# Attention output and its gate kept feature-major through to the output projection

## What is computed

```
h = rmsnorm(x, norm_w) * (1 + scale) + shift;   z = h @ w_in
q_lat, ckv, kr, g_att, u, g_pool = split(z)              # g_att is 512 wide
o[q, head, :] = softmax(q . k, causal) @ v               # 8 heads of 64 values
att = o reshaped to (2048, 512)
mixed = concat(att * silu(g_att), pool(u) * silu(g_pool))   # 1024 wide
y_prompt = rmsnorm(x + gate * (mixed @ w_out), final_norm_w)
```

## Time and profile before

| | us |
|---|---|
| runs (3) | 1607.35, 1608.68, 1615.50 |
| median | 1608.68 |
| span of the profiled execution | 1616.8 |
| PE matmul busy | 1483.7 (92%) |
| DVE, ACT, POOL busy | 780.6, 651.9, 493.5 |

### The profile page before, as it was taken

One profiled execution on the slowest core, in us unless ns is written; L12 is line 12 of the kernel. 1 busy time (PEld: TensorE's weight loads), 2 busy tenths in 40 slices (PEclk: granted clock), 3 DMA queues, 4 the chain that ended last, 5 costly groups with the idle time before them and its releaser, 6 DMA issues. The chain is left out here.

```text
span 1616.8 us, 24423 instructions
## 1 busy us (share of the span) xinstructions
PE 1483.7 (92%) x8584; PEld 1236.4 (76%) x8584; DVE 780.6 (48%) x1594; ACT 651.9 (40%) x1296; POOL 493.5 (31%) x423
## 2 busy tenths in 40 slices
PE   7787799999999589999999999999848999999997
PEld 1487689999998467777777787877627888888886
DVE  0587532223321677766676767664252333333333
ACT  0255322222110556565666666666631222222221
POOL 0355523232221524343443434343331111111100
PEclk9899899999999799999999999999957999999999
DMA  9243221111101200000000000000065144434310
GB/s 367 94 126 110 84 87 53 53 53 52 58 27 47 52 1 11 11 8 12 8 12 8 14 4 14 7 7 11 15 244 181 60 157 156 155 122 146 124 60 28
DMA packets 71502, 114.70 MB, mean 71 GB/s; under 512 B 33236, under 2 KB 50548, under 8 KB 69205
## 3 DMA queue, kind: packets, MB, share of 16 engines
q1 hardware_dynamic: 58782, 70.73, 13.8%
q0 software_dynamic: 3456, 27.26, 4.6%
q10 hardware_dynamic: 9168, 15.50, 2.7%
HBM read 90.95 MB, written 22.77 MB: 70 GB/s over the span
## 5 line engine op out<-in xcount | busy, mean ns | idle before, releaser
L1177 POOL TENSOR_TENSOR pt_lo<-pt,pt_hi 128x512 fp32r<-128x512 f32 (+2 forms) x160 | 171.1, 1069 | 262.3 <-ACT pt_hi L1082 261.9
L1081 ACT ACTIVATE pt<-att_ps_s 128x512 f32<-128x512 f32 (+1 forms) x320 | 170.2, 532 | 150.9 <-PE att_ps_s L1351 85.3
L1237 DVE TENSOR_REDUCE mx<-att_ps_p 128x1 f32<-128x512 f32 (+2 forms) x300 | 177.2, 606 | 91.7 <-PE att_ps_p L1321 71.4
L1082 ACT ACTIVATE pt_hi<-att_ps_s 128x512 fp32r<-128x512 f32 (+1 forms) x320 | 169.2, 529 | 0.0
L1248 DVE TENSOR_TENSOR pt_lo<-pt,pt_hi 128x512 fp32r<-128x512 f32 (+1 forms) x160 | 120.2, 751 | 93.0 <-ACT pt_hi L1082 91.2
L107 PE MATMUL mix_ps_u<-mix_h_hi,wb_hi 128*128 128x256 f32 x512 | 146.2, 285 | 0.0
L109 PE MATMUL mix_ps_u<-mix_h_hi,wb_lo 128*128 128x256 f32 x512 | 144.9, 283 | 0.0
L108 PE MATMUL mix_ps_u<-mix_h_lo,wb_hi 128*128 128x256 f32 x512 | 144.9, 283 | 0.0
L107 PE MATMUL att_ps_o<-pt_hi,v_hi 128*128 128x512 f32 (+1 forms) x320 | 126.9, 397 | 9.3 <-DVE pt_lo L1248 8.5
L107 PE MATMUL out_ps_y<-wo_hi,mixed_hi 128*128 128x512 f32 x256 | 119.4, 466 | 2.6 <-POOL mixed_lo L1938 2.6
L1349 PE MATMUL att_ps_s<-q_hi,k_hi 97*128 97x512 f32 (+1 forms) x320 | 120.3, 376 | 1.6 <-issue 1.6
(11 more groups left out here) (348 smaller groups left out, 3316.2 us busy)
## 6 DMA issues: line engine op xcount, KB each, us to landing
ada<-in_ada_w_dram SPq DMA_DIRECT2D x8, 1536.0 KB, 15.1
lat_x<-in_x_prompt_dram SPq DMA_DIRECT2D x16, 512.0 KB, 4.3
mix_x<-in_x_prompt_dram SPq DMA_DIRECT2D x16, 512.0 KB, 3.7
x_rows<-in_x_prompt_dram SPq DMA_DIRECT2D x16, 512.0 KB
out_dram<-y ACTq DMA_DIRECT2D x16, 512.0 KB, 2.7
lat_wraw<-in_w_in_dram POOLq DMA_DIRECT2D x8, 768.0 KB
gate_att_scratch<-gate_a SPq DMA_DIRECT2D x16, 256.0 KB, 2.0
pool_scratch<-mixed SPq DMA_DIRECT2D x32, 128.0 KB, 2.0
```

The costliest lines, as they stand in the source:

```text
L1081: act.activation(pt[:, k % 2, 0:n], ps_s[:, k % 2, 0:n], ACT.Exp, scale=SCALE)
L1082: act.activation(ph[0][:, k % 4, 0:n], ps_s[:, k % 2, 0:n], ACT.Exp, scale=SCALE).then_inc(exp_done, 1)
L1177: pool.tensor_tensor(ph[1][:, k % 4, 0:n], pt[:, k % 2, 0:n], ph[0][:, k % 4, 0:n].bitcast(F32), ALU.subtract).then_inc(p_lo_ready[1], 1)
L1237: dve.tensor_reduce(mx[:, I % 2, r, c:c + 1], chunk_bank(g, n)[:, 0:width], AX.X, ALU.max).then_inc(chunk_read, 1)
```

## The change

Nothing is transposed back to token-major any more.

- **mix**: `ps_a` becomes feature-major like `ps_u`. The two (token block) groups of 8 x 3 matmuls with 512 moving columns become, per step, 4 groups of 8 x 3 with 256 moving columns. The gate scratch is (4, 128, 2048) and SP writes it in rows of 1 KB.
- **attention**: `turn_out` and `finish` are gone, with their semaphores. `o_cols` has two buffers; ACT copies, after a wait for the store of two groups before, and SP stores 64 rows of values (unnormalised) and the one row of sums, two DMAs, into `att_scratch` (4, 128, 2048) and `den_scratch` (8, 2048). The reuse of the `ps_o` bank waits for ACT's copy.
- **setup**: SP first loads all sums as 128x128 (`s_den`), DVE takes one reciprocal of them, SP writes them back (`rden_scratch`) ahead of its other stores, for which it waits on DVE. The loads of the first block come after that; POOL does two multiplications.
- **output**: per block five DMAs instead of three, all in rows of 512 bytes (attention and pool columns into one tile `raw_cols`, gate columns, and the reciprocals spread over 64 partitions twice). POOL multiplies gate by reciprocal, then attention by that, and makes the whole low part (128x1024); ACT makes the whole high part in one instruction. PE's `turn` and DVE's `low` are gone.

The core of the diff:

```diff
-                    for c in range(KC):
-                        cols = slice(b * P, (b + 1) * P)
-                        last = mm3(pe, ps_a[:, b, :], [hb[0][:, e, c, cols], hb[1][:, e, c, cols]],
-                                   [wb[0][:, c, 0:DATT], wb[1][:, c, 0:DATT]], c == 0, c == KC - 1)
+                    for k in range(2):
+                        cols = slice((2 * b + k) * P, (2 * b + k + 1) * P)
+                        for c in range(KC):
+                            last = mm3(pe, ps_a[:, b, k * T:(k + 1) * T], [wb[0][:, c, cols], wb[1][:, c, cols]],
+                                       [hb[0][:, e, c, :], hb[1][:, e, c, :]], c == 0, c == KC - 1)
...
             def store(h, I):
-                sp.wait_ge(att_ready, NGRP * h + I + 1)
-                sp.dma_start(att_groups[:, I, :, ds(h, 1), :].squeeze(2), att[:, I % 2]).then_inc(att_out[I % 2], 16)
+                sp.wait_ge(ot_ready, NGRP * h + I + 1)
+                cols = slice(I * 512, (I + 1) * 512)
+                sp.dma_start(att_heads[:, ds(h, 1), cols], ot[0:VD, I % 2, :].unsqueeze(1)).then_inc(att_out[I % 2], 16)
+                sp.dma_start(den_heads[:, ds(h, 1), cols], ot[VD:VW, I % 2, :].unsqueeze(1)).then_inc(att_out[I % 2], 16)
...
-                if exists(NGRP * h + I - 1, NGRP * H):
-                    act.wait_ge(ot_turned, NGRP * h + I)
-                act.activation(ot[0:VW, :], ps_o[0:VW, I % 2, :], ACT.Copy).then_inc(ot_ready, 1)
+                if exists(NGRP * h + I - 2, NGRP * H):
+                    act.wait_ge(att_out[I % 2], 32 * (2 * h + I // 2))
+                act.activation(ot[0:VW, I % 2, :], ps_o[0:VW, I % 2, :], ACT.Copy).then_inc(ot_ready, 1)
...
-                    pe.wait_ge(att_ready, NGRP * h + I - 1)
+                    pe.wait_ge(ot_ready, NGRP * h + I - 1)
...
+    def load_cols(eng, raw, gate, rec, cols, landed):
+        eng.dma_start(raw[:, 0:NG, :], att_cols[:, :, cols]).then_inc(landed, 16)
+        eng.dma_start(raw[:, NG:, :], pool_cols[:, :, cols]).then_inc(landed, 16)
+        eng.dma_start(gate[:], gate_att_cols[:, :, cols]).then_inc(landed, 16)
+        for k in range(2):
+            eng.dma_start(rec[k * VD:(k + 1) * VD], rden_pairs[k, :, cols].partition_broadcast(VD)).then_inc(landed, 16)
...
+            sp.dma_start(den[:], den_d.rearrange("h (n s) -> (h n) s", s=P)).then_inc(den_in, 16)
             sp.dma_start(z[:], zs_d).then_inc(z_in, 16)
...
+            sp.wait_ge(rden_ready, 1)
+            sp.dma_start(rden_d.rearrange("h (n s) -> (h n) s", s=P), den[:]).then_inc(rden_out, 16)
             sp.dma_start(o[7].rearrange("a b s c -> (a b) s c")[:, 0:PREV - 1, :], prev[:, 1:, :]).then_inc(out_done, 16)
...
+            dve.wait_ge(den_in, 16)
+            dve.reciprocal(den[:], den[:]).then_inc(rden_ready, 1)
             dve.wait_ge(ss_ready, 1)
...
-            def gated_rows(n, b):
-                pool.wait_ge(r_in[b], 24 * (n - b) + 48)
-                pool.tensor_tensor(ar[b][:], ar[b][:], ga[b][:], ALU.mult).then_inc(gated, 1)
+            def gated_cols(n, b):
+                pool.wait_ge(r_in[b], 16 * LOADS * (n // 2 + 1))
+                pool.tensor_tensor(ga[b][:], ga[b][:], rb[b][:], ALU.mult).then_inc(divided, 1)
+                pool.wait_ge(divided, n)
+                pool.tensor_tensor(raw[b][:, 0:NG, :], raw[b][:, 0:NG, :], ga[b][:], ALU.mult).then_inc(gated, 1)
...
             def low(n, b):
                 pool.wait_ge(hi_ready, n + 1)
-                pool.tensor_tensor(ml[b][:, GRP:, :], pc[b][:], mh[b][:, GRP:, :].bitcast(F32), ALU.subtract).then_inc(lo_pool, 1)
+                pool.tensor_tensor(ml[b][:], raw[b][:], mh[b][:].bitcast(F32), ALU.subtract).then_inc(lo_ready, 1)
```

More of the change, by code:

```diff
@@ L1271, in body @@
                         split(h, k)
-                    end = ended(h, k, LAG + 3)
-                    if end and exists(h + end[0], H):
-                        finish(h + end[0], end[1])
             for c in range(0, NGRP, 2):
@@ L1367, in values @@
                     j == 0, j == GRP * I + GRP - 1).then_inc(pv_done, 1)
-            def turn_out(h, I):
-                pe.wait_ge(ot_ready, NGRP * h + I + 1)
-                for r in range(GRP):
-                    last = pe.transpose(ps_o[:, I % 2, r * VW:(r + 1) * VW], ot[0:VW, r * P:(r + 1) * P], ident[0:VW, 0:VW])
-                last.then_inc(ot_turned, 1)
             def body(h, e):
@@ L2083, in _ @@
         def _(pe):
-            def turn(n, b):
-                pe.wait_ge(gated, n + 1)
-                if exists(n - 1, NB):
-                    pe.wait_ge(lo_att, n)
-                for c in range(GRP):
-                    last = pe.transpose(ps_t[:, c * P:(c + 1) * P], ar[b][:, c * P:(c + 1) * P], ident[:])
-                last.then_inc(turned, 1)
             def unit(n, part, v):
```

112 lines of the change are left out of this document (45 added, 67 removed).

## The result

| | before | changed |
|---|---|---|
| first runs, median | 1612.1 (4 runs) | 1645.9 (4 runs, 1633.2 to 1651.2) |
| ratio, 95% interval | | 1.017 (1.010 to 1.024) |
| later runs, median | 1616.4 (29 runs) | 1623.2 (14 runs, 1613.0 to 1656.8) |
| ratio, 95% interval | | 1.004 (1.001 to 1.007) |
| span of the profiled execution | 1616.8 | 1631.6 |

The forecast was 1598.4. The change does not make the kernel faster; it makes it slower by 0.4 to 1.7%, and it scatters more. (Some executions run longer than the rest at a lower clock; the medians hold them, the ratios leave them out, and without them the later medians are 1614.8 before and 1622.0 changed.) The profiled execution of the changed kernel is the best of its first four runs.

The account below looks back on a forecast made before the run. PE at full clock was taken to bound mix, attention and output; small steps and DMAs the setup. +4.8 - 9.3 - 1.2 - 1.0 + 1.7 + 1.7 - 7.0 + 0 = -10.3 us, giving 1598.4 us, range 1588 to 1609.

Parts of the forecast that it names:

- the first: Mix, attention, output stage: PE is busy at full 2.4 GHz, so removed matmuls shorten the time and added ones lengthen it.
- The closing sentence of the prediction: Whole kernel: a clock falling to 1.2 GHz more often than before would above all make the forecast wrong; no size given.
- Mix: Gate product in mix: 768 matmuls of 256 columns replace 384 of 512, +4.8 us in full.
- From the end of mix to the first scores: Stretch between mix's closing transposes and attention's first scores: no change, 0 us.
- Attention: Attention stage: 31 transpose groups leave PE's stream, -9.3 us; fewer PE waits for DVE, -1.0 us.
- Rival 1: Attention: PE's freed time is lost waiting on each tile's chain; 1608.7 if all but the end, 1603.5 if half; chance 0.16.
- The end of attention and the setup: Last store follows ACT's copy, -1.2 us; setup's extra issue, reciprocal and second POOL multiplication, +1.7 us, bounds 0 and +4.
- Start of the output stage: Output stage's start: POOL's doubled low part and later `out_gate_s` outweigh removed transposes, +1.7 us.
- Turns: Output stage in steady state: removed `turn` transposes save 0.44 us for each of 14, twice that for the first, -7.0 us.
- The shared port: Output stage: DVE's `s_diag` waits for POOL on the shared SBUF port; 0 us taken, bounds -3.0 and +17.
- Rival 2: Output samples, second block: POOL's longer string holds the port and delays DVE and PE, +17 us, 1616; chance 0.16.
- The sum: Whole kernel: all terms together -10.3 us, median from 1608.7 to 1598.4 us.

Follow-up runs that it names:

- experiment 8: Changed kernel with the first output block's five loads in 2 KB rows from other places; last attention matmul to first product 48.9 us against 53.1, one execution.
- experiment 4: Changed kernel with the six thin matmuls that end a sample's values moved from unit 16 to unit 22, in samples 1 to 6; 1676.0 us.
- experiment 2: Kernel before without PE's transposes in the output stage alone, loads and POOL's work as before; 1617.3 us.
- experiment 1: Changed kernel plus four idle transposes behind unit 6 of each of the 16 output blocks; 1617.6 us.
- experiment 15: Changed kernel with one unit of the second block brought forward per sample, without early loads; 1610.1 us, ratio 0.996 to the kernel before.
- 5: Changed kernel with second-block units reordered, two in step 16 and two in step 17, none in steps 30 and 31; 1617.2 us.
- 13: Changed kernel with three first-block loads issued early and one unit brought forward, two in step 16, none in step 31; 1606.5 us, ratio 0.993 to before.
- 6: Changed kernel plus four idle transposes behind each of steps 22 and 28, where PE's stream is wide anyway; 1618.9 us.
- 12: Changed kernel plus eight idle matmuls of 8 columns behind step 28 of samples 0 to 6; 1627.4 us.
- 3: Changed kernel plus seven idle matmuls of 512 columns once, in unit 22 of the first sample; 1631.2 us.
- experiment 9: The changed kernel itself, word for word, run again; 1623.2 us over 14 runs.
- 10: Changed kernel with three of the first output block's five loads issued at about 1171 us instead of 1187; 1622.2 us.
- 7: Changed kernel plus one idle matmul of 512 columns behind each of steps 15, 16 and 17 of samples 0 to 6; 1617.0 us.
- 11: Changed kernel with three first-block loads issued early and second-block units reordered, two in step 16 and two in step 17; 1613.0 us.

## Why the prediction was wrong

**The step that failed** is the first: "each time at the full clock of 2.4 GHz ... So in these three stages a matmul that goes shortens the time by its place in PE's stream". The clock was taken as a given of the stage, read from the windows before. It is an outcome of the stream. The output stage before was at full clock with one fall at a place where PE does little work per time; that row (0.93 in one window of 48 us) was in the trace, and the prediction does not use it. Taking 14 groups of wide transposes out made the stream thinner and the sample shorter, and in the two profiled executions of the changed kernel the clock fell at that place in six and in three samples, in the second of them for 78.5 us in the last sample besides. The clock's share rose by 19.7 us in the median. The closing sentence of the prediction named this, but it stood in no rival and had no price, and the range ended at 1609.

The terms one by one:

- Mix: +4.8 forecast, +4.1 measured.
- From the end of mix to the first scores: 0 forecast, +2.3 measured; 1.7 of it is the clock (20.5 us at half clock before, 23.9 after).
- Attention: -9.3 - 1.0 forecast, -10.2 measured. That the sum fits so well is luck: PE's waits in this stretch fell by 2.2 us (those for maxima from 4.3 to 1.9), not 1.0, so the transposes were worth about 8.0 us, not 9.3. Rival 1 did not come.
- The end of attention and the setup: -1.2 + 1.7 forecast, +3.9 measured. Of the three things the reciprocal was rightly sized (1.1 forecast, 0.94 measured, inside idle time). The wrong sentence is that the first block's loads "have the 15 us or so up to 1205 to hide in". They did hide, but w_out's loads came 4.5 us late because of them (experiment 8, one execution). I had asked only who waits for the moved DMAs, not who shares the DMA engines with them.
- Start of the output stage: +1.7 forecast, +2.0 measured; PE's wait for DVE is 5.91 us, 3.55 before, so `out_gate_s` came later than I took, and the rest went faster.
- Turns: the work went as forecast (7 us), the time did not.
- The shared port: 0 forecast, -2.6 measured, inside the bounds. `s_diag` takes 218 ns in the median now, 1182 before: POOL's low part is done by then, as I read it. Rival 2 did not come in this kernel, but experiment 4 shows that its mechanism is real and one shift away.
- The sum: -10.3 forecast; -11.3 in span times clock, and -10.2 in time once both kernels have the same order of units and neither loses more to the clock than the other. Part of that agreement is luck too: the way from attention to the first product is 3.4 us longer than forecast, and the port gave 2.6 us that were not in the sum.

**What is shown and what stays open.** Shown: the excess lies in the clock (work falls, clock's share rises by 19.7 us); the removal of the transposes alone brings half of it (72.7 against 62.9 in experiment 2); with the new loads and POOL's new string, but PE work put back, 5 us are left (67.9 against 62.9 in experiment 1); a reordering of PE's own work takes it away (65.9 against 64.6 in experiment 15). Not shown is what the chip reacts to. Wide work at the weak place helps (5, 13, 15), wide work elsewhere helps (6), and even thin work that only lengthens the sample stops the runs over 1640 (12). Neither theory explains all of them; a short fall seems to need the weak place and a bad moment, and kernels with the same stream have both kinds of samples. The long fall in the last sample was not studied: no experiment changes that place alone. Not shown either is that the length of the sample matters by itself. Of the 45 runs of kernels that have the transposes out and nothing in their place (first runs, 2, 3, 9, 10), 16 took over 1640 us; of the 88 of the variants that fill or reorder (1, 5, 6, 7, 11, 12, 13, 15), one did, the 1770.6 of experiment 15; of the 120 of the kernel before beside them, nine did, one of them a single run of 6108 us, whose cause is open.

## What to carry to other kernels

Where a stage runs at the full clock, ask how close it is to a fall: look for the places with many small matmuls in a row and for single falls in the windows, and price a removal of wide work near them with up to half a fall's length per pass, not with zero. Profile more than one execution where runs scatter: here two of the same kernel lost their time at different places. Compare two kernels by span times granted clock as well as by time; here it gave 11.3 us where the kernels without the extra loss differ by 10.2, while the time alone said the opposite. And when a load is split into many small rows, look at what else is on the DMA engines then: the load that is late may be another one.

## What the runs showed of the hardware that I had not expected

- TensorE's clock fell with PE busy without a break: 48.00 of 48.00 us busy at a clock of 0.93, 0.84 in the worst window of the first profile, and 0.56 in that of experiment 9, in a stretch of 78.5 us at half clock.
- Idle work on PE can cost nothing: 7 us of transposes of the identity brought the clock's share from 81.1 to 67.9 us, and the median is 1617.6, 1623.2 without them.
- A DVE operation on 1x8 elements lasted 3.62 us, through two POOL operations in a row, not one. The Trainium skill ("SBUF — State Buffer", SBUF: two separate sides) lets the loser wait for the whole of the other's instruction; here it waited for two.
